# A decoder trunk on one core: the first branch's gates in the merged rows' home, half of the second branch's gate sums among the value pages, and short sums made fewer

## The reference, cut to what matters

```python
q_sb, k_sb, v_sb, q_mem, p_rw, g_sb, g_mem, g_rw = _split(x @ w_in, IN_SPLITS)
...
merged = (jax.nn.sigmoid(g_sb) * (o_sb @ w_sb_o) + jax.nn.sigmoid(g_mem) * (o_mem @ w_mem_o)
          + jax.nn.sigmoid(g_rw) * (o_rw @ w_rw_o))
h = _layer_norm(DN_ALPHA * x + merged @ w_out, ln1_g, ln1_b)
y = _layer_norm(DN_ALPHA * h + _moe(h, ...), ln2_g, ln2_b)
```

## Time and profile before

| | us |
|---|---|
| median of 3 runs | 1544.32 |
| lowest, highest | 1536.92, 1550.21 |
| time of the profiled execution | 1544.9 |
| its span, first to last instruction | 1543.0 |
| PE busy in it | 1470.7 (95%) |
| DVE busy | 571.4 (37%) |
| ACT busy, POOL busy | 265.8, 141.4 |

### The profile page before, as it was taken

The page is one execution under the profiler, slowest core; times in us unless marked ns, Lnnn a source line. Parts: engine busy times, 40 slices in busy tenths (PEclk is TensorE's granted clock), DMA queues, the critical chain, the costliest instruction groups (busy, mean ns, idle before and its releaser), DMA issues.

```text
span 1543.0 us, 22210 instructions
## 1 busy us (share of the span) xinstructions
PE 1470.7 (95%) x8378; PEld 747.7 (48%) x8378; DVE 571.4 (37%) x993; ACT 265.8 (17%) x534; POOL 141.4 (9%) x267
## 2 busy tenths in 40 slices
PE   7998979899999999999999999999999999999995
PEld 6886635457877755334334434434434434434431
DVE  2999846744354643221221211211211211211214
ACT  1111522331312211011011011111111111111102
POOL 5322232111210101000000000000000000000000
PEclk9999989999999999999999999999999999999998
DMA  9899988884311274999999999999999999999994
GB/s 344 322 361 341 346 304 324 304 286 142 83 56 56 110 281 174 425 427 428 429 429 428 428 429 429 428 429 428 429 429 429 429 429 428 429 428 428 428 427 171
DMA packets 67897, 534.30 MB, mean 346 GB/s; under 512 B 8587, under 2 KB 9686, under 8 KB 35062
## 3 DMA queue, kind: packets, MB, share of 16 engines
q1 hardware_dynamic: 48774, 471.52, 73.9%
q0 software_dynamic: 8656, 41.97, 7.7%
q10 hardware_dynamic: 10400, 19.92, 3.6%
HBM read 528.92 MB, written 4.46 MB: 346 GB/s over the span
## 4 chain that ended last, share of the span: by engine, by line
PE 82%; DMA 8%; issue 4%; DVE 3%; ACT 2%; POOL 0%; POOLq 0%; DVEq 0%; SPq 0%; ACTq 0%
PE bank L810 79%; PE bank L811 3%; DMA early<-in_w_gate_up 2%; DMA arena<-in_w_gate_up 2%; DMA ring<-in_w_in 1%; DMA arena<-in_state_rw_wkv 1%; DMA ring<-in_w_mem_kv 1%; DMA ring<-in_cache_sb_v 1%; DVE arena L2365 0%; ACT memT L1937 0%; DMA arena<-in_x_sample 0%; POOLq L467 0%; ACT arena L1666 0%; DVE arena L2341 0%; DVE arena L2454 0%
## 5 line engine op out<-in xcount | busy, mean ns | idle before, releaser
L810 PE MATMUL bank<-arena 64*64 64x64 f32 (+9 forms) x2738 | 293.5, 313 | 6.6 <-ACT arena L1952 1.3
L2566 DVE TENSOR_SCALAR arena<-bank 128x256 f32<-128x256 f32 x64 | 27.0, 422 | 628.8 <-PE bank L810 628.8
L810 PE MATMUL bank<-projT,ring 128*128 128x264 f32 x1056 | 253.2, 393 | 4.0 <-DMA ring<-in_w_in 1.6
L810 PEld LDWEIGHTS bank<-arena 64*64 64x64 f32 (+5 forms) x2738 | 186.0, 157 | 127.9 <-issue 114.9
L810 PE MATMUL bank<-ring,projT 128*64 128x512 f32 x1024 | 229.7, 595 | 0.8 <-DMA ring<-in_w_gate_up 0.8
L810 PEld LDWEIGHTS bank<-projT,ring 128*128 128x128 f32 x1056 | 197.1, 191 | 45.1 <-issue 5.0
L810 PE MATMUL bank<-ring,memT 128*64 128x512 f32 (+2 forms) x640 | 168.2, 605 | 5.6 <-ACT memT L1937 4.5
L810 PEld LDWEIGHTS bank<-ring,projT 128*64 128x64 f32 x1024 | 70.6, 137 | 149.9 <-issue 147.9
L810 PE MATMUL bank<-projT 128*64 128x512 f32 (+1 forms) x544 | 118.3, 581 | 0.3 <-DMA projT<-in_w_gate_up 0.3
L1933 ACT ACTIVATE arena<-arena 128x256 f32<-128x256 f32 x64 | 26.7, 417 | 411.0 <-DVE arena L2566 411.0
L810 PEld LDWEIGHTS bank<-ring,memT 128*64 128x64 f32 (+2 forms) x640 | 51.3, 143 | 81.0 <-issue 70.1
(11 more groups left out here) (288 smaller groups left out, 1080.7 us busy)
## 6 DMA issues: line engine op xcount, KB each, us to landing
ring<-in_w_gate_up SPq DMA_DIRECT2D x64, 2048.0 KB, 20.2
projT<-in_w_gate_up SPq DMA_DIRECT2D x32, 2048.0 KB, 21.1
ring<-in_w_down SPq DMA_DIRECT2D x32, 2048.0 KB, 24.6
arena<-in_w_gate_up SPq DMA_DIRECT2D x16, 2048.0 KB, 20.5
projT<-in_w_down SPq DMA_DIRECT2D x16, 2048.0 KB, 23.2
early<-in_w_gate_up SPq DMA_DIRECT2D x16, 2048.0 KB, 22.1
ring<-in_cache_sb_k SPq DMA_DIRECT2D x64, 256.0 KB, 6.4
ring<-in_cache_sb_k POOLq DMA_DIRECT2D x64, 256.0 KB, 5.9
```

The source lines that it names most:

```text
L810: mm = lambda out, l, r, first, last, **k: pe.matmul(out, l, r, start=first, stop=last, **k)
L2566: ts(g_, chunk[:, 0:512:2], LIMIT, None, ALU.min).then_inc(sem("g_ready"), 1)
```

## The change

Both kernels compute the same. In `beside()` the second branch's gate tiles 0 to 3 now come before the first branch's outputs: gates 0 are products 0 to 64, gates 1 low 64 to 96, outputs 0 96 to 128, gates 1 high 128 to 160. 96 products now stand among the value pages, 64 before. The first branch's gate sums and their sigmoid are kept in `mergedT`, and DVE multiplies the outputs straight from their banks (`gated_rows`) where ACT moved them and POOL multiplied. ACT issues the two loads of the second branch's gates; SP loads `("wo", 0)` behind `mV`. `sample_sums` adds two samples at once in two row groups, and `so_sT` joins the groups with the matrix `both`. `ys` is four products of 512 columns and four turns in place of 16 products of 2 columns. The router's sums over eight tiles are added on POOL first. The eight `keep_warm` products among the pages are gone.

```diff
-           ("wo", 0): 1, ("mV", 0): 2, ("mV", 1): 3, ("gate", 1, 0): 0, ("gate", 1, 1): 2, ("wo", 1): 3,
+           ("gate", 1, 0): 1, ("gate", 1, 1): 1, ("mV", 0): 2, ("mV", 1): 3, ("wo", 0): 0, ("wo", 1): 3,
...
-    for kind, br in (("gate", 0), ("o", 0), ("gate", 1), ("o", 1), ("gate", 2)):
-        g += [(kind, br, dt) for dt in range(KT)]
+    low, high = range(4), range(4, KT)
+    for kind, br, tiles in (("gate", 0, low), ("gate", 0, high), ("gate", 1, low), ("o", 0, low), ("o", 0, high),
+                            ("gate", 1, high), ("o", 1, low), ("o", 1, high), ("gate", 2, low), ("gate", 2, high)):
+        g += [(kind, br, dt) for dt in tiles]
...
-            sp.wait_ge(*last_reader(("gate", 0, 1)))
-            load_rows(("wo", 0))
             for i in range(2):
                 for u in (28 + 2 * i, 29 + 2 * i):
                     sp.wait_ge(*last_reader(("V", u)))
                 load_cache(("mV", i))
-            for name, before in ((("gate", 1, 0), ("mK", 1)), (("gate", 1, 1), ("mV", 0)), (("wo", 1), ("mV", 1)),
-                                 (("gate", 2, 0), ("wo", 0)), (("gate", 2, 1), ("gate", 1, 0)),
-                                 (("wo", 2), ("gate", 1, 1)), (("wout", 0), ("wo", 1)), (("wout", 1), ("gate", 2, 0))):
+            for name, before in ((("wo", 0), ("mK", 1)), (("wo", 1), ("mV", 1)), (("wo", 2), ("mV", 0)),
+                                 (("gate", 2, 0), ("gate", 1, 1)), (("gate", 2, 1), ("wo", 0)),
+                                 (("wout", 0), ("wo", 1)), (("wout", 1), ("gate", 2, 0))):
                 sp.wait_ge(*last_reader(before))
                 load_columns(sp, name) if name[0] == "gate" else load_rows(name)
...
-                    if br == 0:
-                        g.tensor_tensor(mergedT[:, dt, :], mergedT[:, dt, :], gate_at(dt), ALU.mult
-                                        ).then_inc(sem("branch_summed"), 1)
-            gated(0, range(KT))
...
+            for m, into in ((bwr, bwr[:, 0:4]), (gwr, bwr[:, 4:8])):
+                link(g.tensor_tensor(into, m[:, 0:4], m[:, 4:8], ALU.add))
+                link(g.tensor_tensor(into[:, 0:2], into[:, 0:2], into[:, 2:4], ALU.add))
+                g.tensor_tensor(into[:, 0:1], into[:, 0:1], into[:, 1:2], ALU.add).then_inc(sem("router_summed"), 1)
...
-            def sample_sum(bq):
-
-                last = mm(b[0:NB, :], pick[:, 7 - bq:15 - bq], pvm[bq % 2], bq == 0, bq == NB - 1)
-                last.then_inc(sem("pv_summed"), 1) if bq < NB - 1 else done("so_s", last)
+            def sample_sums(b0):
+
+                pe.wait_ge(sem("pv_kept"), b0 + 2)
+                b = start("so_s") if b0 == 0 else bank[5]
+                for i in range(2):
+                    bq = b0 + i
+                    last = mm(b[32 * i:32 * i + 32, :], pick[:, 7 - bq:39 - bq], pvm[i], b0 == 0, b0 == NB - 2)
+                last.then_inc(sem("pv_summed"), 2) if b0 < NB - 2 else done("so_s", last)
...
             def low_rank(nm):
+                pe.wait_ge(sem("lora_in"), 48)
+                pe.wait_ge(sem("lora_act"), 2)
...
-                    if t == 0 and nm == "dec":
-                        keep_warm(b, 2)
-                    if t == 0:
-                        pe.wait_ge(sem("lora_in"), 48)
-                        pe.wait_ge(sem("lora_act"), 2)
...
-            def over_heads(nm, src, ready, mat=blk, early=0):
-
+            def over_heads(nm, src, ready, mat=blk):
+
+                pe.wait_ge(sem(ready), 1)
-                    if t == 0:
-                        keep_warm(b, early)
-                        pe.wait_ge(sem(ready), 1)
                     done((nm, t), mm(b[:, 0:src.shape[2]], mat[:], src[:, t, :], True, True))
...
             sample_values(5)
+            branches(24, 28)
             selection_sums(1)
             sample_values(6)
             later_sums(0)
-            branches(24, 28)
+            branches(28, 32)
             sample_values(7)
             later_sums(1)
-            branches(28, 32)
-            sample_sum(0)
+            branches(32, 36)
...
             values(1)
-            sample_sum(1)
-
-            branches(32, 36)
+            sample_sums(0)
+
+            branches(36, 40)
...
-            branches(36, 40)
+            branches(40, 44)
             sample_values(15)
-            sample_sum(2)
...
-            branches(40, 44)
+            branches(44, 48)
             sample_values(16, 17)
             memory_values(0)
-            branches(44, 48)
+            branches(48, 52)
...
             memory_query(2)
             sample_values(19)
+            branches(52, 56)
             low_rank("dec")
             memory_query(3)
-            sample_sum(3)
+            sample_sums(2)
...
             sample_values(21)
             low_rank("gr")
-            branches(48, 52)
+            branches(56, 60)
             memory_values(1)
-            branches(52, 56)
+            branches(60, 64)
             sample_values(22)
             memory_scores(2)
             sample_values(23)
-            sample_sum(4)
...
             over_heads("kn", T1, "kk_sq")
             memory_turn(2)
             memory_query(4)
-            branches(56, 60)
+            branches(64, 68)
             sample_values(24, 25)
             memory_values(2)
             memory_query(5)
-            branches(60, 64)
+            branches(68, 72)
             sample_values(26)
             memory_scores(3)
             sample_values(27)
-            sample_sum(5)
-
-            over_heads("bon", T1, "rk_prod", early=6)
+            sample_sums(4)
+            branches(72, 80)
+
+            over_heads("bon", T1, "rk_prod")
             memory_turn(3)
             memory_query(6)
+            branches(80, 88)
             sample_values(28, 29)
             memory_values(3)
             memory_query(7)
+            branches(88, 96)
             sample_values(30, 31)
-            sample_sum(6)
-            sample_sum(7)
+            sample_sums(6)
             pe.wait_ge(sem("zm"), 1)
...
-            row_to_features("so_sT", "so_s")
+            gone(pe, "so_s")
+            b = start("so_sT")
+            for t in range(4):
+                last = mm(b[:, NB * t:NB * t + NB], orow[0:64, t * P:t * P + P], both[0:64, :], True, True)
+            done("so_sT", last)
...
             gone(pe, "so_sT")
-            branches(64, 72)
+            branches(96, 104)
...
-            branches(80, 112)
+            branches(112, 136)
             pe.wait_ge(sem("state_in"), 16)
...
-            branches(112, 136)
+            branches(136, 148)
             flat = lambda a: a.rearrange("p t b v -> p t (b v)")
             over_heads("sa", flat(S1), "s_kk")
-            branches(136, 148)
             over_heads("vb", flat(S2), "s_v")
             branches(148, 160)
...
             for t in range(4):
+                last = mm(b[32 * t:32 * t + 32, :], blk[:, 0:P:4], S1[:, t].rearrange("p b v -> p (b v)"), True, True)
+            done(("ys", 0), last)
+
+            def state_values_turned():
+
+                gone(pe, ("ys", 0))
+                b = start(("ysT", 0))
                 for bp in range(4):
-                    c0 = 8 * t + 2 * bp
-                    last = mm(b[:, c0:c0 + 2], S1[:, t, 2 * bp:2 * bp + 2, :].rearrange("p b v -> p (b v)"),
-                              blk[:, 0:P:64], True, True)
-            done(("ys", 0), last)
+                    last = tr(b[:, P * bp:P * bp + P], ysr[:, P * bp:P * bp + P])
+                done(("ysT", 0), last)
...
             pe.wait_ge(sem("hats"), 1)
             turned_hats(RW_PARTS[0], "tab")
             turned_hats(RW_PARTS[0], "tkv")
+            state_values_turned()
             for nm in ("g1", "g2"):
                 grams(RW_PARTS[0], nm)
...
-            pe.wait_ge(sem("router_scaled"), 2)
+            pe.wait_ge(sem("router_summed"), 2)
             b = start("router_sums")
-            for i, m in enumerate((gwr, bwr)):
-                for k in range(KT):
-                    last = mm(b[:, NE * i:NE * i + NE], ones[:, :], m[:, k, :], k == 0, k == KT - 1)
+            for i, k in enumerate((4, 0)):
+                last = mm(b[:, NE * i:NE * i + NE], ones[:, :], bwr[:, k, :], True, True)
             done("router_sums", last)
...
                 for dt in tiles:
-                    move(("gate", br, dt), gate_at(dt), lambda b: b[:, 0:T])
+                    move(("gate", br, dt), gate_at(dt) if br else mergedT[:, dt, :], lambda b: b[:, 0:T])
...
                 gone(act, ("gate", br, KT - 1))
-                act.activation(gates, gates, ACT.Sigmoid).then_inc(sem("gates_ready"), 1)
+                at = gates if br else mergedT[:]
+                act.activation(at, at, ACT.Sigmoid).then_inc(sem("gates_ready"), 1)
...
                 values(g4)
+            gate_sums(0, (4,))
             act.wait_ge(sem("arena_clear"), 1)
             memory_weights(0)
-            gate_sums(0, (4,))
             memory_turned(0)
```

(44 more changed lines are left out.)

52 lines of the change are left out of this document (28 added, 24 removed).

## The result

The changed kernel takes 1568.4 us (median of four runs, 1562.4 to 1575.3), the kernel before 1541.7 us (median of four, 1536.9 to 1550.2). The ratio is 1.0167 with a 95% interval from 1.0127 to 1.0206. In five more rounds it was 1.019 (1.015 to 1.0229). The forecast was 1560.1 us, with a range to 1567: the sign and the two large waits were right, but the sum was too small, most of all in the stretch up to "kn".

The account below looks back on a forecast made before the run. The prediction took the expert loop as a fixed-length weight stream, so PE's time before it counts one for one. Terms +7.6, +5.5, +0.9, +15.0, -10.3, +0.3, -3.2 gave +15.8 on 1544.3: 1560.1 us, range 1546 to 1567.

Parts of the forecast that it names:

- the sign: Whole kernel: slower, by +15.8 us; chance of slower by over 1% put at 0.38, faster by over 1% at 0.04.
- the two large waits: PE waits 5.9 us for gates behind `memory_query(4)` and 12.4 us for ("wo", 0), each followed by 2.6 us lost clock.
- Up to 'kn': Stretch ahead of "kn": "dec" at 262.2 instead of 261.87, PE reaches "kn" 0.7 us earlier.
- From "st" to `so_out`: 24 products in place of 48, DVE's update done 17.7 us after "st", PE at 18.0: -10.3 us.
- the state: Ahead of "st": transfer takes 16.2 us from issue, PE waits 5.6 us instead of 1.85; net 0.
- First branch's outputs. 0.: DVE's eight multiplications, about 0.4 us each, hide in its idle gaps; POOL's and ACT's work goes; 0 us.
- The gates in time (A): Load of ("gate", 1, 0) lands in time, DVE late by 1.1 us only: +9.3, 1553.6 us; chance 0.14.
- queues in turns (B): Three queues share bandwidth by thirds, PE waits 3.3 us for the gates instead of 5.9: +13.2, 1557.5 us; chance 0.15.
- the output weights soon (C): PE waits only 4.9 us for ("wo", 0) and keeps most of its clock: +6, 1550.3 us; chance 0.12.
- D, faster: Last 16 products free because DVE and pages set the end of the pages: -6.3, 1538.0 us; chance 0.04.
- F, nothing moves: Loads wait as forecast but the fillers cancel them, +-3: 1544.3 us; chance 0.05.
- E: State transfer beside two output-weight loads, or pages held up by the gates: +22, 1566.3 us; chance 0.08.

Follow-up runs that it names:

- warm_dec: The changed kernel with two `keep_warm` products put back ahead of "dec"; 1563.8 us, ratio 1.0167 to the kernel before.
- combo3: combo, with ACT moving gate tiles 0 and 1 before the third memory weights and SyncE issuing the second and third output weights after the state lands; 1534.0 us.
- combo: The changed kernel with eight gate products behind `memory_scores(3)`, 16 behind `so_sT`, POOL's `s_v` products behind the hats, `keep_warm` products ahead of "dec"; 1543.7 us.
- pool_later: The changed kernel with POOL's four products for `s_v` held back until DVE has set the hats; 1564.3 us, ratio 1.0174 to the kernel before.
- back16: The changed kernel with 16 products of gate tiles 2 and 3, ACT's moves and its gates load moved behind `so_sT`; 1557.6 us, ratio 1.0119 to the kernel before.

## Why the prediction was off, step by step

The terms of the sum against the means of three profiles each, as differences of stretches (differences are taken before rounding; the end of "bon" is the start of its last two products):

| stretch | before | changed | measured | my terms |
|---|---|---|---|---|
| "dec" to "kn" | 20.1 | 22.7 | +2.7 | -0.7 |
| "kn" to the end of "bon" | 26.9 | 36.4 | +9.6 | +8.3 |
| to the end of the pages | 14.5 | 19.0 | +4.5 | +5.5 |
| to "st" | 32.7 | 50.5 | +17.8 | +15.9 |
| "st" to `so_out` | 31.0 | 23.1 | -7.9 | -10.3 |
| to the scan | 10.2 | 9.9 | -0.3 | +0.3 |
| to the expert loop | 212.5 | 208.1 | -4.4 | -3.2 |
| sum | 347.7 | 369.6 | +21.9 | +15.8 |

The forecast missed the median by 8.3 us. Of these 6.1 are terms of the sum from "dec" on, 1.4 the stretch ahead of "dec", -2.6 the level (I built on 1544.3 us, the median with a fourth run is 1541.7), and 3.4 the part by which the medians stand further apart than the profiles.

*Right.* The expert loop did not change. PE waits 5.50 us for the gates behind `memory_query(4)` (I had 5.9) and 14.15 us for `("wo", 0)` (I had 12.4); each is followed by the lower clock. That load took 15.6 us, as I had it (15.3); PE came to it 1.6 us behind its issue, where I had 2.9. The filler products, the router sums and `ys` cost what I had taken from the rows. The waits for the gates were 7.9 and 7.8 us in the two later profiles, so 5.9 was low.

*Wrong, and the largest miss: "Up to 'kn'".* I took four filler products for two `keep_warm` products at an even price, put "dec" 0.3 us later and counted the stretch as a gain of 0.7 us. But ACT's gate move waits for those very products, and the tanh and sigmoid of the low-rank input stand behind it. PE waits 2.57 us, and the work from "dec" to about 267 us runs at the lower clock. That is +2.7 us from "dec" on and +1.4 ahead of it, +4.1 instead of -0.7; warm_dec takes 3.5 us back between "dec" and "kn". The step that failed was to count the instruction that was replaced and not what it stood for: the `keep_warm` products waited with PE.

*Too small: the clock behind each wait.* I charged 2.6 us behind each of the two waits for weights. From "st" to `so_out` I charged none, and the lower clock is there as well: "st" takes 3.23 us where the earlier trace rows show 2.20, and the 24 products behind it 7.73 us where combo3 shows 5.61. That is 3.1 us of lost time in a term that I put at -10.3 and that came out at -7.9. In combo3, where PE waits only 0.15 us ahead of "st", the stretch takes 19.9 us, which is what I had forecast.

*Wrong in its reason, right in its size: the state.* I had it land 16.2 us after its issue and PE wait 5.6 us. It landed after 17.3 us and PE waited 2.82, since DVE's late rows kept PE back for 2.08 us and at the lower clock in between. I had taken the transfer's time as given. combo3 shows that it is not: 7.6 of combo's 18.2 us went with the loads issued ahead of it.

*Wrong without a price: "First branch's outputs. 0."* DVE's eight multiplications are short and hidden, as I said. What I did not look at was POOL: with its work gone, its next four products start 0.3 us ahead of a DVE product and hold it for 3.6 us. pool_later shows the mechanism and no time for it, so this is no part of the miss.

*The rivals.* The gates in time (A), queues in turns (B) and the output weights soon (C) are excluded by the waits of 5.5 to 7.9 us and of 14 us. So are D, faster, and F, nothing moves: the time rose by 26.7 us. E came near in price (1566.3 us) for the wrong place: the state took 16.5 to 17.6 us from its issue, hardly more than the 16.2 before, and no page was held up by the gates.

*Open.* The 3.4 us between profiles and medians, and why the short sums, 3.8 us in the profiles, gain nothing in timed runs.

## What to carry to other kernels

Work that is moved ahead of a load's buffer release moves the load back too: the 16 products among the last pages took PE's time there, and the weights that PE wanted next were issued later (5.4 us later than in back16). Leave ready work behind the point at which a load is issued, and put it into the wait.

Where a wait is short, ask what runs behind it: here 2.6 us of idle time cost some 3.5 us more through the clock. Ask as well whether the engine waited for has to wait for the work just moved. And before one engine is relieved, ask what it will do earlier, and beside whom.

When two profiles are compared, cut away the stretches ahead of the change: they differed by 12 us for almost the same code. But keep the wait just ahead of the first instruction that you count from.

## What the runs showed of the hardware that I had not expected

- PE busy is not PE at full clock. 256 instructions with 32 columns kept PE and PEld busy for 50 us, and the granted clock was 0.54 all the time; 56 with 512 columns had 1.00.
- A DVE product with both inputs in SBUF took 4.86 us beside four products of POOL that took 4.05 us, and 1.22 us without them.
- A transfer of 1 MB on POOL's queue took 16.5 to 18.2 us from its issue with 4.2 MB of weights issued 3 us ahead on SyncE's, and 10.6 us without.
